# The head norm of a differential attention, its mean squares gathered in eight rows of one bank

## The chip, the cores and the metric

One core of one Trainium2 chip. The metric is device time in microseconds for one execution, the median of several runs. Engines: TensorE (PE, matrix products, results in PSUM banks of 128x512 fp32), VectorE (DVE), ScalarE (ACT), GpSimd (POOL, which doesn't read PSUM), SyncE (SP, which issues the weight transfers).

## The reference

A diffusion block of two parts. The second part has two layers; the change lies in the second of them (the "odd" one), a differential attention over 512 positions and 256 context positions, with 8 heads of 128 columns. Cut to what matters:

```
def rms_norm(x, g):
    xf = x.astype(jnp.float32)
    return (xf * lax.rsqrt(jnp.mean(jnp.square(xf), -1, keepdims=True) + RMS_EPS) * g).astype(x.dtype)

def diff_attend(q, k, v, lam, lambda_init, subln_g):
    s = jnp.einsum('bqhtd,bkhtd->bthqk', q, k) * HEAD_DIM ** -0.5
    p = jax.nn.softmax(s, axis=-1)
    a = p[:, 0] - lam * p[:, 1]
    o = jnp.einsum('bhqk,bkhe->bqhe', a, v)          # 512 positions, 8 heads, 128 columns
    o = rms_norm(o, subln_g) * (1.0 - lambda_init)   # the head norm: mean over a head's 128 columns
    return o.reshape(..., 1024)

o_l = diff_attend(...);  out_l = o_l @ w_out
xl = layer_norm(ALPHA * xl + gt1_l * out_l, ln1_g[i], ln1_b[i])
```

## The kernel before

Activations lie transposed: 128 columns on the partitions, positions along the free dimension. So a head's output is one tile `f.O[:, h, :]` of 128x512 fp32, and the mean over its 128 columns is a sum over partitions, made by TensorE with a constant matrix `m128` (128x128, all 1/128) as stationary operand; the result stands alike in all 128 rows of a bank.

Five programs, one for each engine, are written out by hand (`tensor_odd`, `vector_odd`, `scalar_odd`, `pool_odd`; SP has its own). An instruction counts its engine's semaphore up (`up(name)`), others wait for that count (`at(name)`). `everyone(k, eng, stage)` is a barrier: the engine waits until all four have reached the end of `stage`. PSUM banks are handed out in turn by `k.B.take`; a product that takes a bank waits until its last reader is done.

The stages around the change, in order:

- `tensor_attend`, `vector_attend`, `scalar_attend`: 32 units (8 heads of 4 query tiles), a software pipeline three units deep. VectorE takes the maximum (L2112), ScalarE the exponentials (L2183), VectorE the weighted difference (L2136, L2138), TensorE turns it (L280) and multiplies by the values (L259). After a head's fourth unit ScalarE copies its bank to `f.O` (L2201).
- `odat`, a barrier.
- The head norm, key `odn`. ScalarE squares the eight heads into `f.q1` (L2633). TensorE forms eight means, one bank each (`tensor_norms`, fp32, each product two half-products in the trace). VectorE adds EPS from PSUM into `f.k1` (L797), ScalarE takes the root (L2637), VectorE the reciprocal of 128x512 (L802), scales `f.O` by it and by the gain (L2601). ScalarE casts the result to the high half `f.oh[h]` (L2640), VectorE subtracts to get the low half `f.ol[h]` (L2603). VectorE does these last steps head after head.
- The output projection `dout`, eight projections of eight heads each, three fp32r products a head (high by high L253, low by high L254, high by low L255), 24 in all for each. The first waits for head q's halves before its q-th three. After each projection VectorE adds the result to `k.X` (L1835) and TensorE sums the one before for the layer norm's mean (`X,squares`, L259).
- The layer norm of 128x512: mean, variance, L1761 add, L1776 root, L1765 reciprocal, L1785 and L1788 scaling.

Weights go through a ring of six raw tiles; ScalarE casts the high half of each (L235) and GpSimd subtracts the low half (L243), two projections ahead. During the head norm GpSimd does nothing.

```
def project_in(k, pe, name, x, segs, each=None, among=(0, 1, 2, 3, 4, 5)):
    hi, lo = k.W.pair(name)
    pe.wait_ge(k.W.split(name))
...
        for q in range(8):
            if each is not None:
                pe.wait_ge(each(q))
```

Of the kernel before, what the change touches and what calls it, by code (L numbers as in the profile page):

```python
# [8 lines left out]
F = mybir.dt.float32  # L9
# [15 lines left out]
VECS = [("norm1", 8), ("convw", 80), ("convb", 16), ("ssd_norm", 8), ("hyw", 72), ("hyb", 24), ("hbias", 16),  # L25
        ("hy_norm", 8), ("norm2", 8), ("final_norm", 8), ("bmod", 48), ("dtb", 1), ("hyb1", 1), ("hyb2", 1),
        ("fr0", 1), ("fr1", 1), ("ln1g", 16), ("ln1b", 16), ("ln2g", 16), ("ln2b", 16), ("fcw", 132),
        ("fcb", 44), ("bmod2", 96), ("qn", 2), ("kvn", 1), ("subln", 1), ("c1", 16)]
ROWS = [("alog", 32), ("dskip", 16), ("sink", 8), ("lq1", 64), ("lk1", 64), ("lq2", 64), ("lk2", 64), ("i16", 16)]

SEG2, SEG1 = [(0, 512), (512, 768)], [(0, 512)]
# [226 lines left out]
def mm(e, out, w, x, first=True, last=True):  # L258
    return e.matmul(out, w, x, start=first, stop=last, skip_group_check=True)  # L259
# [23 lines left out]
def everyone(k, eng, stage):  # L283

    eng.wait_ge(k.P.at("end", stage), k.V.at("end", stage), k.A.at("end", stage), k.G.at("end", stage))
# [506 lines left out]
def vector_norms(k, dv, key, groups, out, finish, tiles=None):  # L792
    tiles = tiles or (2 if key == "ssdn" else 1)
    for g in range(groups):
        r = out[:, 512 * g:512 * g + 512]
        dv.wait_ge(k.P.at(key, tiles * g + tiles - 1))
        dv.e.tensor_scalar(r, k.B.of((key, g)), EPS, None, ALU.add).then_inc(*k.V.up(key, "ms", g))  # L797
        k.B.over((key, g), k.V.now())
    for g in range(groups):
        r = out[:, 512 * g:512 * g + 512]  # L800
        dv.wait_ge(k.A.at(key, "sqrt", g))
        dv.e.reciprocal(r, r).then_inc(*k.V.up())  # L802
        dv.wait_ge(k.V.now())
        finish(g, r)

# [1360 lines left out]
            values(i - 3)  # L2168


def scalar_attend(k, ac, at, prepare=None):
    e, P, V, A, B, key = ac.e, k.P, k.V, k.A, k.B, at.key
    N, nP = len(at.units), len(at.P)

# [21 lines left out]
    def values(i):  # L2196
        u = at.units[i]
        if u.last:
            ob = B.of((key, "o", u.key))[u.p0:u.p0 + u.rows, 0:u.width]
            ac.wait_ge(P.at(key, "o", i))  # L2200
            e.copy(u.out[0] if isinstance(u.out, tuple) else u.out, ob).then_inc(*A.up(key, "o", i))  # L2201
            B.over((key, "o", u.key), A.now())

    for i in range(N + 3):
        if prepare and i < N:
# [333 lines left out]
def tensor_odd(k, pe):  # L2539
# [23 lines left out]
    pe.wait_ge([G.at("rot", ("d", j)) for j in range(16)], A.at("Vd", 1, 5))  # L2563
    tensor_attend(k, pe, f.at, lambda i: None)
    P.name("end", "odat")
    everyone(k, pe, "odat")
    tensor_norms(k, pe, "odn", 8, 1, lambda n: f.q1[:, 512 * n:512 * n + 512], k.sq["m128"])
    tensor_residual(k, pe, "res1", "dout", lambda q, s: (f.oh[q], f.ol[q]), SEG1, f.P[1:3], lambda q: V.at("odn", "f", q))
    P.name("end", "res1")


def vector_odd(k, dv):
# [21 lines left out]
    everyone(k, dv, "odin")  # L2594
    vector_attend(k, dv, f.at)
    V.name("end", "odat")
    everyone(k, dv, "odat")

    def finish(h, r):
        o = f.O[:, h, :]  # L2600
        e.scalar_tensor_tensor(out=o, in0=o, scalar=k.sub, in1=r, op0=ALU.mult, op1=ALU.mult).then_inc(*V.up("odn", "o", h))  # L2601
        dv.wait_ge(A.at("odn", "oh", h))
        e.tensor_tensor(f.ol[h], o, f.oh[h].bitcast(F), ALU.subtract).then_inc(*V.up("odn", "f", h))  # L2603

    vector_norms(k, dv, "odn", 8, f.k1, finish)
    vector_residual(k, dv, "res1", "dout", m, 16, SEG1)
    V.name("end", "res1")

# [1 line left out]
def scalar_odd(k, ac):  # L2610
# [15 lines left out]
            B.over(("Vd", hf, c), A.now())  # L2626
    A.name("end", "odin")
    everyone(k, ac, "odin")
    scalar_attend(k, ac, f.at)
    A.name("end", "odat")  # L2630
    everyone(k, ac, "odat")
    for n in range(8):
        e.square(f.q1[:, 512 * n:512 * n + 512], f.O[:, n, :]).then_inc(*A.up("odn", "sq", n))  # L2633
    for g in range(8):
        r = f.k1[:, 512 * g:512 * g + 512]
        ac.wait_ge(V.at("odn", "ms", g))
        e.activation(r, r, AF.Sqrt).then_inc(*A.up("odn", "sqrt", g))  # L2637
    for h in range(8):
        ac.wait_ge(V.at("odn", "o", h))
        e.copy(f.oh[h], f.O[:, h, :]).then_inc(*A.up("odn", "oh", h))  # L2640
# [4 lines left out]
def pool_odd(k, po):  # L2645
    e, W, G, f = po.e, k.W, k.G, k.od
    pool_gain(k, po, "ff0", 768, k.vec["ln2g"][:, 0:8], k.vec["ln2b"][:, 0:8])
    everyone(k, po, "ff0")
    e.dma_start(f.rope, k.d["rope"][:, 1024:2048]).then_inc(*k.rope1l.up())
    W.lo(po, ("dqk", 0))  # L2650
    po.wait_ge(k.rope1l.at())
    for j in range(16):
        if j:
            W.lo(po, ("dqk", j))
        dst = f.q[:, j, :] if j < 8 else f.k[:, j - 8, :]
        pool_rotate(k, po, ("d", j), dst[:, 0:512], f.rope[:, 0:512], f.tmp)
    for j in range(8):
        W.lo(po, ("dv", j))
    G.name("end", "odin")
    everyone(k, po, "odin")  # L2660
    G.name("end", "odat")
    everyone(k, po, "odat")
    for j in range(8):
        W.lo(po, ("dout", j))
    G.name("end", "res1")
# [10 lines left out]
def _cols(v):  # L2676

    return np.ascontiguousarray(np.asarray(v).reshape(-1, 128).T)
# [85 lines left out]
def _arrays(p):  # L2764
# [27 lines left out]
    def taps(w):  # L2792
# [11 lines left out]
         "fcw": np.concatenate([taps(p["ffn_conv_w_2"][i]) for i in range(2)], 1), "fcb": _cols(p["ffn_conv_b_2"]),  # L2804
         "bmod2": _cols(p["b_mod_2"]), "qn": _cols(p["mla_q_norm_2"]), "kvn": _cols(p["mla_kv_norm_2"]),
         "subln": _cols(p["diff_subln_g_2"]), "c1": c2(p["c"], p["c_ctx"])}
    a["vecs"] = np.concatenate([v[n] for n, _ in VECS], 1)
    r = {"alog": p["ssd_a_log"], "dskip": p["ssd_d"], "sink": p["swa_sink_2"], "lq1": p["diff_lam_q1_2"],
         "lk1": p["diff_lam_k1_2"], "lq2": p["diff_lam_q2_2"], "lk2": p["diff_lam_k2_2"],
# [301 lines left out]
```

## Time and profile before

| | us |
|---|---|
| median of 3 runs | 5046.19 (5045.71 to 5047.88) |
| the profiled execution | 5075.65 |
| its span | 5073.8 |
| busy: PE, DVE, ACT, POOL | 4531.9, 2722.1, 1515.6, 1754.2 |
| end of attention's last products to the last three products of projection 0 | 4538.15 to 4590.92 |

The profiled execution takes 0.6% longer than those without a profile. Times in rows are from the start of its span. A TensorE that is called busy isn't one at its peak: the granted clock (1.00 is 2.4 GHz, 0.50 is 1.2 GHz) says how fast its products ran.

### The profile page before, as it was taken

What the parts mean: (1) busy time and instruction counts of PE and PEld (TensorE: products, weight loads), DVE (VectorE), ACT (ScalarE), POOL (GpSimd) and SP (SyncE); (2) the same over time, 40 slices, a digit from 0 to 9 for tenths busy, and PEclk for the clock granted to TensorE, in tenths of its full rate; (3) what the DMA queues carried; (4) which work ended last, traced back from release to release, by engine and by line L of the source; (5) the groups of instructions that cost most, each with busy time, mean ns of one, the idle gap of its engine ahead of it and who ended that gap; (6) DMA issues with size and microseconds to landing.
All of it is one profiled execution on the core that took longest, in us unless ns stands there. A gap on an engine that the chain in (4) does not pass through costs nothing.

```text
span 5073.8 us, 51551 instructions
## 1 busy us (share of the span) xinstructions
PE 4531.9 (89%) x20654; PEld 3503.6 (69%) x20654; DVE 2722.1 (54%) x4692; ACT 1515.6 (30%) x2546; POOL 1754.2 (35%) x933
## 2 busy tenths in 40 slices
PE   7866988787669999999999979997999979986998
PEld 3755845356557888888888856666888857754886
DVE  3875745349887666654443334563443450485334
ACT  3211211034752222222222233443212122343222
POOL 2243432025964444444444421003223225102442
PEclk9987999898789999999999999988999989998999
DMA  5210200121235544444433210001122202101331
GB/s 203 96 67 31 92 29 17 62 72 46 117 155 197 171 161 166 164 155 166 171 136 121 100 37 16 13 1 50 55 63 63 63 29 63 34 1 54 92 96 49
DMA packets 170618, 440.76 MB, mean 87 GB/s; under 512 B 12203, under 2 KB 78955, under 8 KB 167436
## 3 DMA queue, kind: packets, MB, share of 16 engines
q1 hardware_dynamic: 168060, 422.61, 24.5%
q0 software_dynamic: 2320, 14.86, 0.8%
q8 instruction: 164, 2.69, 0.2%
q14 instruction: 74, 0.61, 0.0%
HBM read 401.77 MB, written 35.65 MB: 86 GB/s over the span
## 4 chain that ended last, share of the span: by engine, by line
PE 60%; DVE 7%; ACT 2%; issue 1%; DMA 0%; POOL 0%; DVEq 0%; ACTq 0%; POOLq 0%
PE psum L253 17%; PE psum L255 17%; PE psum L254 17%; PE psum L259 7%; DVE st L2112 2%; PE psum L280 1%; DVE Pd L2138 1%; DVE k L802 1%; DVE X L1785 0%; ACT P L2183 0%; DVE ffl L1725 0%; DVE Pe L2136 0%; DVE rstd L1765 0%; DVE X L1788 0%; DVE st L2119 0%
## 5 line engine op out<-in xcount | busy, mean ns | idle before, releaser
L243 POOL TENSOR_TENSOR pair<-raw_ring,pair 128x1024 fp32r<-128x1024 f32 (+1 forms) x503 | 1243.8, 2488 | 2297.2 <-ACT pair L235 2297.1
L235 ACT CAST pair<-raw_ring 128x1024 fp32r<-128x1024 f32 (+1 forms) x503 | 510.3, 1044 | 370.7 <-PE psum L255 321.7
L253 PE MATMUL psum<-pfh,pair 128*128 128x512 f32 x1152 | 460.0, 399 | 27.4 <-POOL pair L243 25.8
L1578 DVE SCALAR_TENSOR_TENSOR h<-psum,mods,h 128x512 f32<-128x512 f32 x512 | 373.0, 748 | 184.4 <-PE psum L255 182.9
L255 PE MATMUL psum<-pfh,pair 128*128 128x512 f32 x1152 | 458.8, 398 | 0.0
L254 PE MATMUL psum<-pfl,pair 128*128 128x512 f32 x1152 | 458.4, 398 | 0.0
L253 PE MATMUL psum<-ffh,pair 128*128 128x512 f32 (+1 forms) x1056 | 382.3, 362 | 45.3 <-DVE ffl L1725 45.3
L253 PE MATMUL psum<-Ah,pair 128*128 128x512 f32 x1024 | 408.6, 399 | 9.8 <-DVE h L1578 4.8
L255 PE MATMUL psum<-Ah,pair 128*128 128x512 f32 x1024 | 407.9, 398 | 0.0
L254 PE MATMUL psum<-Al,pair 128*128 128x512 f32 x1024 | 407.8, 398 | 0.0
L254 PE MATMUL psum<-ffl,pair 128*128 128x512 f32 (+1 forms) x1056 | 380.3, 360 | 0.0
L255 PE MATMUL psum<-ffh,pair 128*128 128x512 f32 (+1 forms) x1056 | 379.8, 360 | 0.0
L1636 ACT ACTIVATE gl<-psum 128x512 f32<-128x512 f32 x122 | 73.1, 599 | 832.6 <-PE psum L255 832.6
L1571 DVE TENSOR_TENSOR pr<-gl,Gb 128x512 f32<-128x512 f32 x128 | 91.4, 714 | 342.2 <-ACT gl L1636 324.3
L253 PEld LDWEIGHTS psum<-pfh,pair 128*128 128x128 f32 x1152 | 218.7, 190 | 79.3 <-issue 23.1
L259 PE MATMUL psum<-o,o 128*128 128x128 f32 x1024 | 177.1, 339 | 101.6 <-POOL o L1503 77.2
L253 PEld LDWEIGHTS psum<-ffh,pair 128*128 128x128 f32 x1056 | 200.6, 190 | 84.1 <-issue 39.1
L254 PEld LDWEIGHTS psum<-pfl,pair 128*128 128x128 f32 x1152 | 218.8, 190 | 50.5
L255 PEld LDWEIGHTS psum<-pfh,pair 128*128 128x128 f32 x1152 | 218.6, 190 | 50.5
L259 PEld LDWEIGHTS psum<-o,o 128*128 128x128 f32 x1024 | 161.4, 243 | 117.6 <-POOL o L1503 78.5
L1948 DVE SCALAR_TENSOR_TENSOR X<-psum,mods,X 128x512 f32<-128x512 f32 (+1 forms) x264 | 170.8, 661 | 121.0 <-PE psum L255 121.0
L253 PEld LDWEIGHTS psum<-Ah,pair 128*128 128x128 f32 x1024 | 194.4, 190 | 56.3 <-issue 9.6
(517 smaller groups left out, 9305.0 us busy)
## 6 DMA issues: line engine op xcount, KB each, us to landing
raw_ring<-wmod SPq DMA_DIRECT2D x144, 512.0 KB, 5.2
raw_ring<-peeru SPq DMA_DIRECT2D x128, 512.0 KB, 4.2
raw_ring<-peerv SPq DMA_DIRECT2D x128, 512.0 KB, 4.8
gates<-stage SPq DMA_DIRECT2D x16, 2048.0 KB, 6.4
Gb<-gates SPq DMA_DIRECT2D x32, 1024.0 KB, 9.2
raw_ring<-win SPq DMA_DIRECT2D x48, 512.0 KB, 4.4
raw_ring<-wgate SPq DMA_DIRECT2D x44, 512.0 KB, 3.5
raw_ring<-wup SPq DMA_DIRECT2D x44, 512.0 KB, 3.6
```

Of the source, the lines that this page charges most:

```text
L235: ac.e.copy(self.pair(t)[0], k.R.of(t)).then_inc(*k.A.up("hi", t))
L243: po.e.tensor_tensor(lo, k.R.of(t), hi.bitcast(F), ALU.subtract).then_inc(*k.G.up("lo", t))
L253: e.matmul(out, w[0], x[0], start=first, stop=False, skip_group_check=True)
L254: e.matmul(out, w[0], x[1], start=False, stop=False, skip_group_check=True)
L255: return e.matmul(out, w[1], x[0], start=False, stop=last, skip_group_check=True)
L259: return e.matmul(out, w, x, start=first, stop=last, skip_group_check=True)
L280: return e.transpose(out, src, k.sq["ident"][0:n, 0:n])
L1571: e.tensor_tensor(v3(y, 32), v3(x, 32), G4[:, :, n % 4, :], ALU.mult).then_inc(*V.up("act", n))
L1578: e.scalar_tensor_tensor(out=h[:, j, :], in0=B.of(("down", gi, j)), scalar=m[:, 40 + j, 0:1], in1=h[:, j, :], op0=ALU.mult, op1=ALU.add).t ...
L1636: e.activation(gelus(k, n), B.of((("U", n), 0)), AF.Gelu).then_inc(*A.up("gelu", n))
L1948: e.scalar_tensor_tensor(out=x, in0=B.of((key, "down", gi, q, s))[:, 0:b - a], scalar=m[:, 40 + q, s:s + 1], in1=x, op0=ALU.mult, op1=ALU. ...
L2112: e.tensor_reduce(s[:, 0:1], bank[:, 0:u.n], AX, ALU.max).then_inc(*V.up())
```

## The change

The mean squares of the eight heads are gathered in one bank. The stationary operand for head h is a window of 8 columns out of a table `z128` (128x15, 1/128 in column 7, else 0), so that the sum lands in row h and adds nothing to the other rows; eight products accumulate into 8x512. Then one add, one root and one reciprocal of 8x512 instead of eight each of 128x512. A second product for each head brings row h back to all 128 rows: its stationary operand is column h of the first eight rows of the unit matrix, broadcast to 128 columns (8x128). VectorE scales `f.O` straight from that bank. The low half of odd heads goes to GpSimd. The squares of a head are issued in the attention's loop, behind the head's copy. The barrier `odat` falls. The means and the products with ones take banks 0 to 5. The constants `z64`, `z256`, `z128` add 52 columns to the transfer of `vecs`; only `z128` is read.

```diff
+def tensor_means(k, pe, key, n, sq, place, rows, among=(0, 1, 2, 3, 4, 5, 6, 7)):
+    bank = k.B.take((key, "ms"), 1, among)
+    pe.wait_ge(k.B.free((key, "ms")))
+    for i in range(n):
+        pe.wait_ge(k.A.at(key, "sq", i))
+        mm(pe.e, bank[0:rows, :], place(i), sq(i), i == 0, i == n - 1).then_inc(*k.P.up(key, "sq", i))
+
+def vector_means(k, dv, key, n, rows, out):
+    dv.wait_ge(k.P.at(key, "sq", n - 1))
+    dv.e.tensor_scalar(out[0:rows, :], k.B.of((key, "ms"))[0:rows, :], EPS, None, ALU.add).then_inc(*k.V.up(key, "ms"))
+    k.B.over((key, "ms"), k.V.now())
+
+def scalar_means(k, ac, key, rows, out):
+    ac.wait_ge(k.V.at(key, "ms"))
+    ac.e.activation(out[0:rows, :], out[0:rows, :], AF.Sqrt).then_inc(*k.A.up(key, "sqrt"))
+
+def vector_inverse(k, dv, key, rows, out):
+    dv.wait_ge(k.A.at(key, "sqrt"))
+    dv.e.reciprocal(out[0:rows, :], out[0:rows, :]).then_inc(*k.V.up(key, "inverse"))
+
+def tensor_back(k, pe, key, g, w, out, among=(0, 1, 2, 3, 4, 5, 6, 7)):
+    bank = k.B.take((key, "back", g), 1, among)
+    pe.wait_ge(k.V.at(key, "inverse"), k.B.free((key, "back", g)))
+    mm(pe.e, bank, w, out).then_inc(*k.P.up(key, "back", g))

@@ scalar_attend, in values(i), at a head's last unit
             B.over((key, "o", u.key), A.now())
+            if square:
+                square(u.key)

@@ tensor_odd
-    everyone(k, pe, "odat")
-    tensor_norms(k, pe, "odn", 8, 1, lambda n: f.q1[:, 512 * n:512 * n + 512], k.sq["m128"])
-    tensor_residual(k, pe, "res1", "dout", lambda q, s: (f.oh[q], f.ol[q]), SEG1, f.P[1:3], lambda q: V.at("odn", "f", q))
+    tensor_means(k, pe, "odn", 8, lambda h: f.q1[:, 512 * h:512 * h + 512], lambda h: k.vec["z128"][:, 7 - h:15 - h], 8, SIX)
+    for h in range(8):
+        tensor_back(k, pe, "odn", h, k.sq["ident"][0:8, h:h + 1].to_broadcast([8, 128]), f.k1[0:8, 0:512], SIX)
+    tensor_residual(k, pe, "res1", "dout", lambda q, s: (f.oh[q], f.ol[q]), SEG1, f.P[1:3], lambda q: (G if q % 2 else V).at("odn", "f", q))

@@ vector_odd
-    everyone(k, dv, "odat")
-
-    def finish(h, r):
+    vector_means(k, dv, "odn", 8, 8, f.k1[:, 0:512])
+    vector_inverse(k, dv, "odn", 8, f.k1[:, 0:512])
+
+    def second(h):
+        dv.wait_ge(A.at("odn", "oh", h))
+        e.tensor_tensor(f.ol[h], f.O[:, h, :], f.oh[h].bitcast(F), ALU.subtract).then_inc(*V.up("odn", "f", h))
+
+    for h in range(8):
         o = f.O[:, h, :]
-        e.scalar_tensor_tensor(out=o, in0=o, scalar=k.sub, in1=r, op0=ALU.mult, op1=ALU.mult).then_inc(*V.up("odn", "o", h))
-        dv.wait_ge(A.at("odn", "oh", h))
-        e.tensor_tensor(f.ol[h], o, f.oh[h].bitcast(F), ALU.subtract).then_inc(*V.up("odn", "f", h))
-
-    vector_norms(k, dv, "odn", 8, f.k1, finish)
+        dv.wait_ge(P.at("odn", "back", h))
+        e.scalar_tensor_tensor(out=o, in0=o, scalar=k.sub, in1=B.of(("odn", "back", h)), op0=ALU.mult, op1=ALU.mult).then_inc(*V.up("odn", "o", h))
+        B.over(("odn", "back", h), V.now())
+        if h % 2:
+            second(h - 1)

@@ scalar_odd
-    scalar_attend(k, ac, f.at)
+
+    def square(h):
+        ac.wait_ge(A.now())
+        e.square(f.q1[:, 512 * h:512 * h + 512], f.O[:, h, :]).then_inc(*A.up("odn", "sq", h))
+
+    scalar_attend(k, ac, f.at, square=square)
     A.name("end", "odat")
-    everyone(k, ac, "odat")
-    for n in range(8):
-        e.square(f.q1[:, 512 * n:512 * n + 512], f.O[:, n, :]).then_inc(*A.up("odn", "sq", n))
-    for g in range(8):
-        r = f.k1[:, 512 * g:512 * g + 512]
-        ac.wait_ge(V.at("odn", "ms", g))
-        e.activation(r, r, AF.Sqrt).then_inc(*A.up("odn", "sqrt", g))
+    scalar_means(k, ac, "odn", 8, f.k1[:, 0:512])

@@ pool_odd
-    everyone(k, po, "odat")
+    for h in range(1, 8, 2):
+        po.wait_ge(k.A.at("odn", "oh", h))
+        e.tensor_tensor(f.ol[h], f.O[:, h, :], f.oh[h].bitcast(F), ALU.subtract).then_inc(*G.up("odn", "f", h))
     for j in range(8):
         W.lo(po, ("dout", j))

@@ constants
+        ("z64", 30), ("z256", 7), ("z128", 15)]
+    v["z128"] = np.tile(np.arange(15) == 7, (128, 1)) / 128.0
```

## Rows read from the trace of the kernel before

**Rows 1.** The page: shares of the chain that ended last, by engine.
```profile
PE 60%; DVE 7%; ACT 2%; issue 1%; DMA 0%; POOL 0%; DVEq 0%; ACTq 0%; POOLq 0%
```

**Rows 2.** Chain of waits, 4500 to 4660 us: start, length, engine, tile, line.
```profile
4535.46 2.69 PE psum L259 x24
4538.18 0.59 ACT O L2201
4538.86 0.64 ACT q L2633
4539.63 7.12 PE psum L259 x16
...
4547.47 3.27 DVE k L802
4550.76 0.76 DVE O L2601
4551.55 0.63 ACT oh__32736_512_387 L2640
4552.19 0.69 DVE ol L2603
...
4590.92 0.79 PE psum L253
...
4592.56 0.43 PE psum L253
...
4599.86 0.86 PE psum L259 x2
...
4606.30 0.86 PE psum L259 x2
...
4649.72 0.70 DVE rstd L1761
...
4651.11 3.35 DVE rstd L1765
```

**Rows 3.** Windows: length, then busy PE, PEld, DVE, ACT, POOL; PEclk; DMA.
```profile
4551.00:4553.00 2.00, 0.00 (x0) 0.00 (x0) 1.32 (x3) 0.62 (x1) 0.00 (x0) 0.71 0.00 0
4596.00:4597.00 1.00, 1.00 (x5) 0.78 (x5) 0.00 (x0) 0.00 (x0) 0.49 (x1) 0.89 0.73 287
4653.00:4660.00 7.00, 0.00 (x0) 0.00 (x0) 6.92 (x10) 5.40 (x7) 2.75 (x3) 0.59 0.00 0
40.30:45.50 5.20, 5.20 (x7) 0.85 (x8) 2.98 (x9) 0.90 (x1) 0.00 (x0) 0.50 0.08 31
4663.00:4672.00 9.00, 3.85 (x7) 2.16 (x8) 8.96 (x5) 3.41 (x5) 9.00 (x5) 0.50 0.43 123
```

**Rows 4.** Timeline of ScalarE, in the attention and at the kernel's end.
```profile
4526.66 0.60 ACT L2201 COPY O<-psum 128x512 f32<-128x512 f32 x1
4528.92 0.90 ACT L2183 ACTIVATE Pd<-psum,st 128x768 f32<-128x768 f32 x1 [1.66 <-DVE st L2119]
...
5056.40 1.28 ACT L1776 ACT_TABLE_LOAD   x1
5058.32 0.63 ACT L1776 ACTIVATE rstd<-rstd 128x512 f32<-128x512 f32 x1 [0.64 <-DVE rstd L1761]
```

**Rows 5.** Timeline of TensorE, 0 to 45 us; "128*2" is the stationary operand.
```profile
40.30 5.28 PE L259 MATMUL psum<-raw_ring,vecs 128*2 128x512 f32 x6 [5.59 <-ACT vecs L495]
```

**Rows 6.** Groups of instructions, DVE and POOL: count, busy us, mean ns.
```profile
L2155 DVE TENSOR_TENSOR efl<-psum,efh 64x512 fp32r<-64x512 f32 x16 | 11.0, 689 | 20.8 <-ACT efh L2201 20.8
...
L2232 POOL TENSOR_TENSOR k<-k,rope 128x512 f32<-128x512 f32 x8 | 10.3, 1293 | 34.2 <-PE psum L259 34.2
...
L243 POOL TENSOR_TENSOR pair<-raw_ring,pair 128x1024 fp32r<-128x1024 f32 (+1 forms) x503 | 1243.8, 2488 | 2297.2 <-ACT pair L235 2297.1
```

**Rows 7.** Transfers by issuing queue: KB each, us to landing.
```profile
vecs<-vecs POOLq DMA_DIRECT2D x1, 328.5 KB, 8.8
```

**Rows 8.** Timeline of VectorE, 4660 to 4680 us.
```profile
4662.98 8.97 DVE L1725 TENSOR_TENSOR ffl<-hid,ffh 128x512 fp32r<-128x512 f32 x4
```

More of the change, by code:

```diff
@@ L27 @@
         ("fr0", 1), ("fr1", 1), ("ln1g", 16), ("ln1b", 16), ("ln2g", 16), ("ln2b", 16), ("fcw", 132),
-        ("fcb", 44), ("bmod2", 96), ("qn", 2), ("kvn", 1), ("subln", 1), ("c1", 16)]
+        ("fcb", 44), ("bmod2", 96), ("qn", 2), ("kvn", 1), ("subln", 1), ("c1", 16),
+        ("z64", 30), ("z256", 7), ("z128", 15)]
 ROWS = [("alog", 32), ("dskip", 16), ("sink", 8), ("lq1", 64), ("lk1", 64), ("lq2", 64), ("lk2", 64), ("i16", 16)]
@@ L2168, in vector_attend, with scalar_attend @@
             values(i - 3)
-def scalar_attend(k, ac, at, prepare=None):
+def scalar_attend(k, ac, at, prepare=None, square=None):
     e, P, V, A, B, key = ac.e, k.P, k.V, k.A, k.B, at.key
@@ L2806, in _arrays @@
          "subln": _cols(p["diff_subln_g_2"]), "c1": c2(p["c"], p["c_ctx"])}
+    p2 = np.arange(128)[:, None] // 64
+    v["z64"] = (np.arange(30)[None] == 14 + p2) / 64.0
+    v["z256"] = np.tile(np.arange(7) == 3, (128, 1)) / 256.0
+    v["z128"] = np.tile(np.arange(15) == 7, (128, 1)) / 128.0
     a["vecs"] = np.concatenate([v[n] for n, _ in VECS], 1)
```

## The prediction

> **What bounds the kernel now.** I read the page first: TensorE carries 60% of the chain over the whole span [rows 1], so a change to one norm matters most where TensorE stands still. The chain of waits from 4535 to 4660 us shows such a place [rows 2]. The last products of attention end at 4538.15 (4535.46 + 2.69). Then come the copy of O, the squares, sixteen half-products of means (7.12), and eight rounds, one a head, of reciprocal 3.27, scaling 0.76, cast 0.63 and subtraction 0.69 on the chain; they begin at 4547.47, and at 4590.92, 5.43 us a round later, the last three products of projection 0 begin (they need head 7). From the end of attention's products to 4590.92 are 52.8 us, 1% of the span, and VectorE's reciprocals hold more than half of them. The windows then show what TensorE's clock did [rows 3]: full (2.4 GHz) through the means, granted half (1.2 GHz) from about 4551.8 (0.71 mean in 4551 to 4553), and full again at about 4596.2 (0.89 in 4596 to 4597), 5.3 us after gapless work began.
>
> **The change part by part.** Each sum is measured from the end of attention's products.
>
> *Squares in attention.* Seven of eight move into the loop. After the copy of O at the end of a head (0.60) ScalarE stands 1.66 us before the next exponential [rows 4]. The wait for its own copy (0.09 between 4538.77 and 4538.86 [rows 2]) and the square (0.64) take 0.73 of it, 0.93 are left: nothing on the path. If that cover were gone, seven times 0.73 would cost 5 us. The eighth square ends at 4539.5.
>
> *Means.* TensorE need not stand for the first square: the eight products follow attention's at once, and the eighth square is there long before the eighth product is. That is 7.12 instead of 8.59 (4546.74 − 4538.15). The stationary matrix has 8 columns instead of 128, but the products stream 512 columns; the nearest row, stationary matrices of 2 columns, took 0.88 us a half-product at half clock [rows 3, 5], twice the 0.445 of the means at full clock [rows 2]. So a narrow matrix saves nothing.
>
> *One add, one root, one reciprocal.* From the add to the start of the reciprocal the layer norm took 1.39 us, and the reciprocal 3.35 (4649.72 to 4654.46 [rows 2]). With 0.03 to start: 4.77. Are eight rows cheaper than 128? A subtraction over 64 partitions took 689 ns [rows 6], as long as the 0.69 over 128 [rows 2]: time goes by columns. I take 3.35; the other end, 3.1 us less, stays for the range. The load of the Sqrt table, 1.28 us, is issued ahead of the wait: at the kernel's end it ran at 5056.40, before the root was released at 5058.32 [rows 4]. Here it lies beside the means. Its cost if it came behind the wait: 1.28.
>
> *Products with ones.* Eight more fp32 products of 512 columns. TensorE starts 0.06 after the reciprocal; the first takes about 1.0 at full clock, hand-over 0.1: 1.2 us. At 0.89 each the rest stay ahead of VectorE, which needs 0.76 for a scaling and, for each pair, 0.69 for one subtraction. The six banks suffice: the seventh product waits for the first scaling only.
>
> *Scalings and subtractions.* On VectorE 8 × 0.76 + 3 × 0.69 = 8.2 until head 7 is scaled. Its cast: 0.67. Then GpSimd's subtraction: 0.1 to start (hand-overs in rows 2 take 0.03 to 0.09), 1.29 by the nearest row [rows 6], 0.05 to TensorE: 1.4.
>
> Sum: 7.12 + 4.77 + 1.2 + 8.2 + 0.67 + 1.4 = 23.4 against 52.8: **29.4 us less**.
>
> *Clock in the first two projections.* Before, 27 products took 8.94 us (4590.92 to 4599.86); at full clock 24 take 6.44 − 0.86 = 5.58, and 27 take 6.3 [rows 2]. After the change TensorE has worked almost without gap for 11 us by then, so it should be at full clock: 2.6 less, of which I keep 0.2 for a product's start: 2.4.
>
> *Where work is moved past.* GpSimd now has four subtractions ahead of the low halves of `dout`. That for projection 2 (2.49 [rows 6]) begins at about 23.6 and ends at 26; TensorE needs it at 23.4 + 6.3 + 0.9 = 30.6. Nothing. ScalarE's casts keep their place behind `oh`. Behind the new wait of the root stand the casts `oh`, which need its result anyway; behind the seventh product with ones stands projection 0, which needs all eight; the barrier `odat` that falls held nobody but TensorE and the squares. SP's queue is not touched; no transfer ran in the norm. The vectors grow by 52 columns, 26 KB, at the start: 328.5 KB landed in 8.8 us [rows 7], so at most 0.7 later for what is behind them; I take 0.1, since the larger x lies between them and the first product.
>
> *DVE and GpSimd at once.* While GpSimd worked (9 of 9 us [rows 3]), four subtractions of two SBUF tiles took 8.97 us, 2.24 each instead of 0.69 [rows 8]. Here VectorE's subtraction starts right behind the odd scaling and ends 0.69 later; GpSimd's begins 0.8 after the scaling and ends at 2.1; the next subtraction on VectorE is due at 0.69 + 1.52 = 2.2. They miss each other narrowly. I take 0; three full collisions would cost 3.9.
> The Trainium skill, SBUF — State Buffer, "SBUF: two separate sides", calls this an exclusive lock that a VectorE instruction with two SBUF inputs and a GpSimd one hold for their whole length, the other being blocked. The trace agrees (2.24 against 0.69); scaling from PSUM has one SBUF input and would be free of it. The rule speaks against this edit, and by it the sum would be the same as long as the two alternate as above.
>
> Total: 29.4 + 2.4 − 0.1 for the start of the kernel = 31.7; the narrow miss on the shared port may cost 0.1 a pair, so I take **31.4 us**. The profiled execution took 5075.65 us (span 5073.8, 1.85 around it), 0.6% over the 5046.19 median; scaled, 31.4 is 31.2. Forecast: 5015.0 us.
>
> **Rivals.**
> 1. *The clock is half when the products with ones begin.* TensorE stands 4.8 us ahead of them (7.12 to 11.95). The clock fell 5.1 us after the means ended, and 4.6 us after the layer norm's last product (0.59 over 4653 to 4660 [rows 3]), on both sides of 4.8. At half clock a product takes 1.7 [rows 5], three fit into the 5.3 us [rows 3], and the third scaling is 1.9 us late. Gain 29.3: 5017.
> 2. *The clock stays half through all eight*: 13.7 us of products, the last scaling 5.2 later, and the 2.2 of the projections gone. Gain 24: 5022. Against it: 4596.2 came 5.3 us after gapless work began. For it: no product with 8 rows is in the trace.
> 3. *VectorE and GpSimd collide*: three times 1.29. Gain 27.5: 5018.7.
> 4. *Reciprocal, root and add are cheaper on eight rows*: gain 34.5: 5011.8.
> 5. *Squares force a change of tables in the loop.* Two loads of 1.28 and 0.73 against 1.66 of idle time: 1.63 a head, 11.4 over seven. Gain 20: 5026. Against it: squares ran 0.09 us after the copy, behind exponentials, and a load came only before Sqrt [rows 2, 4].
> The Trainium skill, ScalarE: Activation LUTs, "What ACT_TABLE_LOAD costs", puts a switch at 1283 ns plus a drain of about 1380. The load agrees (1.28); with the drain this rival would take some 30 us and cancel the gain. No drain is seen here.
> 6. *Slower: half clock through the whole output projection.* A product with 8 of 128 rows may not bring the clock back, and nothing after it would. Half clock costs 0.43 against 0.2325 a product [rows 2]: 15 more in projection 1 (+3.0), six projections (+28.4), eight means and eight variances at +0.86 each (+13.8), rival 2's 5.2: +50 against 29.3, 5067 us. It decides if the clock is still half in about the fifth projection, after some 60 us of such work; the trace had 5.3.
> 7. *The gain is given back later* (weights late, another stage's clock): within 0.2%. The slack of 4.6 us above speaks against it.
>
> **How the numbers follow.** Chances: forecast 0.44, rival 1 0.28, rival 2 0.06, rival 3 0.08, rival 4 0.05, rival 5 0.03, rival 6 0.02, rival 7 0.04. About 0.2% (10 us) is what a measurement of this kernel tells from no change. Faster by more: forecast and rivals 1 to 5, 0.94; within: 0.04; slower: 0.02. The range 5011 to 5020 takes in the forecast and rivals 1, 3 and 4, 0.85 in all, with the runs' scatter of about 1 us at each end; rival 2 lies outside.
>
> **What would show it.** In the profile after: eight squares among the exponentials, the next exponential still released by VectorE; eight mean products right behind attention's; one reciprocal of 8x512, 3.35 us; the windows' clock over the eight products with ones, and their spacing (0.86 or 1.7); VectorE's four subtractions 0.69 each; GpSimd's four near 1.3; `dout`'s last three products some 23 us behind attention's end; projection 1 at 0.23 a product. The prediction is wrong if attention's loop is longer, if products with ones set the pace of the scalings, or if GpSimd's last subtraction is late.

## The result, and the profile after

| us | before | after |
|---|---|---|
| median, range (4 runs each) | 5047.03 (5045.71 to 5048.19) | 4990.72 (4984.73 to 4993.35) |
| ratio, 95% interval | | 0.9883 (0.9870 to 0.9896) |
| the profiled execution, its span | 5075.65, 5073.8 | 4993.35, 4991.5 |

The medians lie 56.3 us apart, 1.12%; by the ratio, which isn't formed from these two medians alone, the gain is 1.17%, 59 us. Gains in us below are differences of medians. The forecast was 5015.0, a gain of 31.2; 4990.72 lies outside its range of 5011 to 5020. The direction was right, the size was not. What follows shows that the 56.3 are two things: some 23 us from the head norm, less than forecast, and over 30 us from a move of most tiles by 192 bytes, which the prediction did not see.

In the kernel after, lines stand 1 to 43 further down than before: the products are L254 to L256 and L260, the reciprocal is L832, the scaling L2644. The chain of waits of the kernel after, around the norm (start, length, engine, tile, line), answers to [rows 2]:

```profile
4480.95 9.90 PE psum L260 x40
4490.87 0.69 DVE k L821
4491.58 0.64 ACT k L827
4492.24 3.35 DVE k L832
4495.63 14.02 PE psum L260 x16
4509.65 0.72 PE psum L254
4510.37 0.43 PE psum L255
...
4515.07 0.43 PE psum L254
4515.49 0.27 PE psum L255
4516.68 0.23 PE psum L254
```

Attention's last product ends at 4483.86, and its end is the zero of all stage times below. The eight means follow it at once inside the piece of 9.90 us. Then come add, root and one reciprocal, 4.76 us together. Instead of eight rounds with a reciprocal each there is one block of 14.02 us: the eight products with ones, at 1.75 us each. They, not VectorE's scalings, set the pace, and the products of projection 0 behind them still take 0.43 us each until about 4515.3, then 0.23.

Windows of the kernel after (columns as in [rows 3]; the column behind POOL's is the granted clock):

```profile
4485.00:4491.00 6.00, 5.83 (x14) 1.08 (x12) 0.13 (x1) 1.43 (x2) 0.00 (x0) 1.00 0.00 0
4491.00:4495.60 4.60, 0.00 (x0) 0.00 (x0) 3.88 (x2) 0.63 (x1) 0.00 (x0) 0.93 0.00 0
4495.60:4509.60 14.00, 13.97 (x17) 5.17 (x17) 7.04 (x10) 4.32 (x7) 3.80 (x3) 0.50 0.00 1
4509.60:4515.30 5.70, 5.70 (x15) 4.44 (x15) 1.35 (x2) 2.62 (x4) 3.66 (x2) 0.50 0.00 0
4515.50:4518.00 2.50, 2.50 (x12) 2.05 (x12) 0.00 (x0) 0.00 (x0) 0.00 (x0) 1.00 0.69 205
```

The clock is full through the means, whose stationary operand has 8 columns and all 128 rows. It falls late in TensorE's pause, about 4 us after the means (0.93 is the mean over 4.6 us of which the last part is at half). It is then half for 14.0 us although TensorE is busy for 13.97 of them, and comes back only after 5.7 us of the projection.

Timelines of ScalarE, VectorE and GpSimd of the kernel after (start, length, line, operation, out and in, in brackets the idle time before and who ended it). ScalarE:

```profile
4471.11 0.60 ACT L2235 COPY O<-psum 128x512 f32<-128x512 f32 x1
4471.74 0.63 ACT L2674 ACTIVATE q<-O 128x512 f32<-128x512 f32 x1
4473.37 0.90 ACT L2217 ACTIVATE Pd<-psum,st 128x768 f32<-128x768 f32 x1 [1.00 <-DVE st L2153]
...
4485.16 1.28 ACT L827 ACT_TABLE_LOAD   x1
4491.58 0.63 ACT L827 ACTIVATE k<-k 8x512 f32<-8x512 f32 x1 [5.13 <-DVE k L821]
```

VectorE:

```profile
4490.87 0.68 DVE L821 TENSOR_SCALAR k<-psum 8x512 f32<-8x512 f32 x1 [9.46 <-PE psum L260]
4492.24 3.34 DVE L832 RECIPROCAL k<-k 8x512 f32<-8x512 f32 x1 [0.69 <-ACT k L827]
...
4499.45 0.75 DVE L2644 SCALAR_TENSOR_TENSOR O<-O,sub,psum 128x512 f32<-128x512 f32 x1 [0.96 <-PE psum L260]
4500.11 0.68 DVE L2639 TENSOR_TENSOR ol<-O,oh__32784_512_387 128x512 fp32r<-128x512 f32 x1
```

GpSimd:

```profile
4504.34 1.27 POOL L2705 TENSOR_TENSOR ol<-O,oh__34320_512_390 128x512 fp32r<-128x512 f32 x1 [2.06 <-ACT oh__34320_512_390 L2681]
```

The square in attention's loop is hidden: the next exponential is still released by VectorE, with 1.00 us left of 1.66 [rows 4]. The load of the Sqrt table lies beside the means and nobody waits for it. The reciprocal on 8 rows costs what it costs on 128, 3.35 [rows 2]. Each scaling waits for a product with ones. VectorE's subtraction takes 0.68 and GpSimd's 1.27: they do not meet.

The norm and its wait are over by 4516. The other part of the gain is not in this stage at all. In windows of 500 us in the middle of the first part, where nothing of the change runs, TensorE is busy all the time at full clock in both kernels. Before:

```profile
2000.00:2500.00 500.00, 500.00 (x2145) 405.00 (x2144) 284.07 (x397) 139.56 (x179) 225.01 (x88) 1.00 0.48 162
```

After:

```profile
2000.00:2500.00 500.00, 500.00 (x2208) 414.01 (x2207) 287.86 (x404) 143.57 (x184) 235.53 (x93) 1.00 0.50 169
```

The same products come 63 more often in the same time: 233.1 ns from one to the next before, 226.4 after. Part of that distance is the execution that was profiled before: at 5075.65 it is 29 us longer than that kernel's median. The first experiment's control separates this.

### The profile page after: what moved, and what is told of

Same layout as the page of the kernel before. It is cut to its first block, busy times and chain, and to the rows that moved or that the text cites. A ratio compares the mean times of both kernels' runs of the same rounds, so it can differ in the third digit from the quotient of the medians.

```text
span 4991.5 us, 51556 instructions
## 1 busy us (share of the span) xinstructions
PE 4475.2 (90%) x20670; PEld 3489.7 (70%) x20670; DVE 2688.9 (54%) x4674; ACT 1512.0 (30%) x2539; POOL 1759.2 (35%) x937
## 4 chain that ended last, share of the span: by engine, by line
PE 60%; DVE 7%; ACT 2%; issue 1%; DMA 0%; POOL 0%; DVEq 0%; ACTq 0%; POOLq 0%
PE psum L254 17%; PE psum L255 17%; PE psum L256 17%; PE psum L260 7%; DVE st L2146 2%; PE psum L281 1%; DVE Pd L2172 1%; DVE X L1819 0%; ACT P L2217 0%; DVE ffl L1759 0%; DVE Pe L2170 0%; DVE rstd L1799 0%; DVE X L1822 0%; DVE st L2153 0%; DVE efl L2189 0%
## 5 line engine op out<-in xcount | busy, mean ns | idle before, releaser
L254 PE MATMUL psum<-pfh,pair 128*128 128x512 f32 x1152 | 451.7, 392 | 27.1 <-POOL pair L244 26.1
L256 PE MATMUL psum<-pfh,pair 128*128 128x512 f32 x1152 | 449.5, 390 | 0.0
L254 PE MATMUL psum<-ffh,pair 128*128 128x512 f32 (+1 forms) x1056 | 377.3, 357 | 45.7 <-DVE ffl L1759 45.7
L254 PE MATMUL psum<-Ah,pair 128*128 128x512 f32 x1024 | 400.8, 391 | 10.2 <-DVE h L1612 4.9
L256 PE MATMUL psum<-Ah,pair 128*128 128x512 f32 x1024 | 400.0, 391 | 0.0
L256 PE MATMUL psum<-ffh,pair 128*128 128x512 f32 (+1 forms) x1056 | 376.3, 356 | 0.0
L254 PEld LDWEIGHTS psum<-pfh,pair 128*128 128x128 f32 x1152 | 217.2, 189 | 73.6 <-issue 22.5
L260 PE MATMUL psum<-o,o 128*128 128x128 f32 x1024 | 173.8, 335 | 104.7 <-POOL o L1537 75.5
L254 PEld LDWEIGHTS psum<-ffh,pair 128*128 128x128 f32 x1056 | 200.6, 190 | 82.9 <-issue 39.1
L256 PEld LDWEIGHTS psum<-pfh,pair 128*128 128x128 f32 x1152 | 217.1, 188 | 45.4
L260 PEld LDWEIGHTS psum<-o,o 128*128 128x128 f32 x1024 | 158.7, 239 | 120.2 <-POOL o L1537 78.2
L254 PEld LDWEIGHTS psum<-Ah,pair 128*128 128x128 f32 x1024 | 193.4, 189 | 51.6 <-issue 10.6
```

The source lines that it names most:

```text
L254: e.matmul(out, w[0], x[0], start=first, stop=False, skip_group_check=True)
L256: return e.matmul(out, w[1], x[0], start=False, stop=last, skip_group_check=True)
```

## The experiments

Two questions: where do the 33 us come from that the norm can't give, and what does the norm give by itself? Beside each of them the kernel before ran on the same chip, with medians of 5046.61 to 5047.95 us over 11 to 21 executions. Not all experiments had the same chip, so each ratio is to the kernel before beside it.

### The control, and the 52 columns alone

*Control: the kernel before, unchanged.*

> The kernel before, unchanged, for a profile on the same chip as the runs beside it. Ratio 1.000. The first profile of it took 5075.65 us, 29 over the median of the runs without one. If that excess belonged to that one execution, this profile takes 5045 to 5050, and products of 512 columns in the experts' stage are spaced less than the 0.2333 us of the first profile, nearer to the 0.2267 of the changed kernel. If it belongs to the profile, it takes 5070 to 5080 again.

Measured: 5053.31 us (8 runs), ratio 1.0009 (0.9986 to 1.0033). Its own profiled execution took 5047.48 us and has this window:

```profile
2000.00:2500.00 500.00, 500.00 (x2186) 410.29 (x2185) 287.45 (x402) 141.42 (x181) 234.03 (x92) 1.00 0.50 170
```

That is 228.7 ns a product. So two profiled executions of the kernel before have two product spacings, 229 ns (5047 us) and 233 ns (5075 us), and the one profiled for the prediction was the slower. The spacing of the kernel after, 226.4, is below both.

This execution, whose span is 5045.6 us, can be laid beside that of the kernel after (4991.5). Timelines of the control: TensorE's last products of attention, and VectorE's add behind the variance of the layer norm.

```profile
4507.15 2.84 PE L259 MATMUL psum<-PTd,Vd 128*128 128x128 f32 x24
...
4621.55 0.69 DVE L1761 TENSOR_SCALAR rstd<-psum 128x512 f32<-128x512 f32 x1 [4.27 <-PE psum L259]
```

The same add in the kernel after:

```profile
4572.90 0.69 DVE L1795 TENSOR_SCALAR rstd<-psum 128x512 f32<-128x512 f32 x1 [4.26 <-PE psum L260]
```

Attention's products end at 4509.99 in the control and at 4483.86 in the kernel after: 26.1 us are gained before the new norm has begun. From there to the add it is 111.56 against 89.04, 22.5 us less, and behind it 5.5 us less. That is the whole difference of 54.1 us, split without any further kernel.

*The 52 columns without the norm.* The new norm is left out; only the constants are added, which nobody reads.

```diff
-        ("fcb", 44), ("bmod2", 96), ("qn", 2), ("kvn", 1), ("subln", 1), ("c1", 16)]
+        ("fcb", 44), ("bmod2", 96), ("qn", 2), ("kvn", 1), ("subln", 1), ("c1", 16),
+        ("z64", 30), ("z256", 7), ("z128", 15)]
```

> The kernel before with nothing of the change but the 52 more columns of constants, which move every tile behind them by 48 columns (192 bytes a partition). Theory A (the head norm gained only about 22 us, the rest of the 56 comes from the new places of the tiles): 5047 - 34 = 5013, ratio 0.993, and the experts' products are closer together than in the control. Theory B (all of the gain comes from the head norm and from what follows it): 5047, ratio 1.000.

Measured: 5005.56 us (5 runs, 5003.17 to 5022.0), ratio 0.9914 (0.9885 to 0.9942): 42.4 us less, from columns that are transferred and not read. Its window:

```profile
2000.00:2500.00 500.00, 500.00 (x2208) 414.01 (x2206) 287.51 (x404) 143.60 (x184) 235.57 (x93) 1.00 0.50 169
```

The products are as dense as in the kernel after. The constants lie first in SBUF, and the base of the tiles behind them is rounded up, so these move up by 48 columns (192 bytes a partition). The raw tiles and the weight pairs hang from the other end and stay.

*The move without the columns.*

```diff
+    m.at += 48          # ahead of k.base = m.at
```

> The kernel before with its tiles moved by the same 48 columns, but with the constants' transfer as it was (no more bytes, no other places in HBM). Theory A with SBUF addresses as its cause: as the kernel with 52 more columns, ratio 0.993. Theory A with the placement in HBM as its cause: ratio 1.000, and only the kernel with more constants gains. Theory B: ratio 1.000.

Measured: 5016.09 us (5 runs), ratio 0.9924 (0.9899 to 0.9949); 2207 products in the same window. Nothing but addresses in SBUF differs from the kernel before, so the place is the cause of this gain, and neither the transfer nor its contents. Whether the columns add anything to it isn't told: the intervals of the two kernels overlap.

*The norm without the move.* The kernel after, with `z128` taken at the end of the odd layer's tiles and written by GpSimd, and no columns added to `vecs`.

```diff
-        ("z64", 30), ("z256", 7), ("z128", 15)]
+    f.z128 = m.take("z128", 15)
...
+    e.memset(f.z128, 0.0).then_inc(*G.up())
+    po.wait_ge(G.now())
+    e.memset(f.z128[:, 7:8], 1.0 / 128).then_inc(*G.up("z128"))
```

> The changed kernel with every tile at its old place: the table of the windows is filled by two memsets of GpSimd at the start of the odd layer, in free columns behind its tiles, and the three new constants are not transferred. Theory A: the head norm's own gain alone, 5047 - 22 = 5025, ratio 0.9956. Theory B: as the changed kernel, 4991, ratio 0.988.

Measured: 5025.13 us (9 runs), ratio 0.9950 (0.9934 to 0.9965). The norm alone gains 22.8 us (25 by the ratio), with an interval of 18 to 33 us (0.35% to 0.66% of 5048). The execution that was profiled, 5060.44 us, is its slowest, and has the long spacing, as the one before:

```profile
2000.00:2500.00 500.00, 500.00 (x2144) 405.02 (x2143) 283.77 (x396) 139.62 (x179) 226.25 (x89) 1.00 0.48 161
```

Its stage is that of the kernel after: products with ones from 11.77 to 25.78 us behind attention, half clock from 10.7 to 31.2. Move alone and norm alone sum to 31.9 + 22.8 = 54.7 or, with the other kernel that has only the move, 42.4 + 22.8 = 65.2. The 56.3 measured for both lies between. With nothing left over beyond the scatter, move and norm together account for the gain.

### Which distance, and between what?

The move shifts most tiles, but not the ring of weight pairs `pair`, which hangs from the other end of SBUF. So the distance between a product's stationary operand (`pair`) and its moving operand (`Ah`, `Al`, `pfh`, `pfl`) changes, as it does to every other tile that moved. That can be reached from the other side: leave all tiles and move only the pairs down by 48 columns.

```diff
-        m.at = 53184 - 6 * 1024 - 2048 * (s + 1)
+        m.at = 53184 - 6 * 1024 - 2048 * (s + 1) - 48
```

> The kernel before with only the weight tiles (the eight pairs of high and low halves) moved, 48 columns down, so that weights and moving operands stand as far apart as in the kernel moved by 48 columns, but every moving operand in its old place. Theory F (the moving operand's own address): spacing stays 0.2292 in the experts' stage, ratio 1.000. Theory H (the distance between the two operands of a product): spacing 0.2267, ratio 0.993.

Measured: 5010.89 us (2 runs), ratio 0.9919 (0.9888 to 0.9950). The window:

```profile
2000.00:2500.00 500.00, 500.00 (x2207) 414.17 (x2206) 287.33 (x405) 143.39 (x184) 235.59 (x93) 1.00 0.51 169
```

The gain is there with no activation moved. So what counts is how far the pairs lie from the tiles behind the constants. The groups by shape in this window show which instructions the gain is in. The control, whose spacing is the usual one of the kernel before:

```profile
L254 PE MATMUL psum<-pfl,pair 128*128 128x512 f32 x360 | 141.8, 394 | 0.0
L253 PE MATMUL psum<-pfh,pair 128*128 128x512 f32 x361 | 141.5, 392 | 0.0
L255 PE MATMUL psum<-pfh,pair 128*128 128x512 f32 x361 | 140.1, 388 | 0.0
```

The kernel with the pairs moved (its other groups read 389 too):

```profile
L253 PE MATMUL psum<-pfh,pair 128*128 128x512 f32 x368 | 143.2, 389 | 0.0
```

The same products, fp32r of 512 columns, have means of 394, 392 and 388 ns, 391 together, against 389 (their length in the pipeline, which is more than the distance to the next). There is no idle time in either; the products themselves are 2 ns shorter on average.

*Only the activations of the first part moved*: `Ah`, `Al` and their neighbours, by 48 columns; `pfh` and `pfl` stay.

```diff
-    m.at = low
+    m.at = low + 48
```

> The kernel before, with only the second set of tiles of the experts' stage moved by 48 columns (Ah, Al, gl, pr, Gb, crow, junk), every other tile in its old place. Theory F (the spacing of products goes by the address of the moving operand): products of Ah and Al are spaced 0.2267 us, those of pfh and pfl stay at 0.229 to 0.233; 3072 products by 2.6 to 6.7 ns, 8 to 20 us won, ratio 0.996 to 0.998. Theory G (something common to the whole kernel shifted with the base): ratio 1.000 and no spacing changes.

Measured: 5049.87 us (8 runs), ratio 1.0004 (0.9994 to 1.0015), 2191 products in the window against the control's 2186. By the starts in the timelines of that window, products that read `Ah` and `Al` came every 227.7 ns on average instead of 228.9, and those that read `pfh` and `pfl` every 229.2 instead of 228.9. That is half of the way to 226.6, and no gain shows in the whole. If only the distance between a product's own two operands counted, those of `Ah` and `Al` should have come at 226.6. So that the moving operand is the tile that matters is supported in part and not shown.

### The period

Every kernel below is the kernel before with the tiles behind the constants moved by so many columns of 4 bytes; constants, raw tiles and pairs stay. The expectations were written in three groups, each when the results of the group before were known.

> The kernel before with all tiles behind the constants moved by 16 columns (64 bytes a partition), so that they begin on a multiple of 128 bytes, as with 48 columns. Theory F1 (what counts is the place modulo 128 bytes): as with 48 columns, spacing 0.2267, ratio 0.993. Theory F2 (it goes by a larger distance): another spacing.

> The kernel before with all tiles behind the constants moved by 32 columns (128 bytes a partition). 16 columns made it slower (1.0037) and 48 faster (0.992). If the spacing goes down steadily with the shift, 32 is in between, near 1.000; if it goes by a residue modulo 128 bytes it is as without a shift, 1.000 with 0.2292; anything else says that a larger distance counts.

> The kernel before with all tiles behind the constants moved by 80 columns, so that they begin on a multiple of 1024 bytes a partition. If good places are those on large powers of two: spacing 0.2267 or less and ratio 0.992 or less. If 80 is a place like any other: between 0.992 and 1.004, and the gain at 48 was luck.

> The kernel before with all tiles behind the constants moved by 40 columns (160 bytes a partition). So far 0 columns gave 2186 products in the window 2000 to 2500 us, 16 and 32 gave 2153 and 2145, 48 gave 2207, 80 gave 2153. If 48 is the middle of a broad good range: 2190 or more and a ratio under 0.997. If it is a narrow one (48 alone): about 2150, ratio 1.001 to 1.004.

> The same with 56 columns (224 bytes). Broad good range: 2190 products or more, ratio under 0.997. Narrow: about 2150, ratio above 1.

> The same with 64 columns (256 bytes). If the spacing repeats every 256 bytes: as without a shift, 2186 (or 2145 in the slower of its two kinds of execution), ratio 1.000. If it doesn't, anything else; below 0.992 it would be a better place than the change's.

> The same with 112 columns, 48 + 64. If the spacing repeats every 256 bytes: as with 48, 2207 products, ratio 0.992. If not, the good distance is one place in a longer pattern; between 0.992 and 1.004.

| moved by | median, us (runs) | ratio (95%) | products in 2000 to 2500 us |
|---|---|---|---|
| 0 (control) | 5053.31 (8) | 1.0009 (0.9986 to 1.0033) | 2186 |
| 16 | 5065.55 (8) | 1.0037 (1.0027 to 1.0048) | 2153 |
| 32 | 5058.33 (8) | 1.0014 (1.0002 to 1.0027) | 2145 |
| 40 | 5076.79 (3) | 1.0057 (1.0035 to 1.0080) | 2145 |
| 48 | 5016.09 (5) | 0.9924 (0.9899 to 0.9949) | 2207 |
| 56 | 5088.09 (2) | 1.0084 (1.0054 to 1.0113) | 2145 |
| 64 | 5048.15 (8) | 1.0004 (0.9993 to 1.0015) | 2186 |
| 80 | 5065.43 (8) | 1.0028 (1.0015 to 1.0040) | 2153 |
| 112 | 5013.43 (3) | 0.9914 (0.9862 to 0.9966) | 2207 |

The pairs (0, 64), (16, 80) and (48, 112) agree, in products and nearly in time: over the distances run, what counts repeats with 64 columns, 256 bytes. A period of 128 bytes would have made 16 like 48, and it costs 0.4% where 48 gains 0.8%. Inside the period 48 is narrow: 40 and 56, 32 bytes to each side, are the slowest, 0.6% and 0.8% over the kernel before. The window of the slowest, moved by 56:

```profile
2000.00:2500.00 500.00, 500.00 (x2145) 401.65 (x2144) 284.39 (x396) 137.90 (x177) 225.56 (x89) 1.00 0.48 163
```

and of that moved by 112:

```profile
2000.00:2500.00 500.00, 500.00 (x2207) 414.15 (x2207) 287.70 (x404) 143.64 (x184) 235.51 (x93) 1.00 0.51 169
```

As means over the window, 500 us by the count, three ranges of spacing appear: 226.6 ns (48, 112, the pairs moved), 228.7 (0, 64) and 232.2 to 233.1 (16, 32, 40, 56, 80). The count of this one window doesn't order the slow kernels: 32, 40 and 56 have 2145 each and lie 30 us apart, so something outside this window adds to it.

### The clock in the norm

Two edits to the kernel after, alone and together. *Filler*: five products of squares by `m128` into a bank that nobody reads, between the means and the products with ones, so that TensorE's pause is filled.

```diff
+def warm(k, pe, key, x, n):
+    bank = k.B.take((key, "warm"), 1, SIX)
+    pe.wait_ge(k.B.free((key, "warm")))
+    for i in range(n):
+        mm(pe.e, bank, k.sq["m128"], x)
+    k.B.over((key, "warm"))
...
+    warm(k, pe, "odn", f.q1[:, 0:512], 5)
```

> The changed kernel with five more products of 512 columns (m128 by the squares, into a bank that nobody reads) between the means and the wait for the reciprocal; 4.3 us of work in a gap of 4.8. Theory C (the clock fell in the gap and the eight-row products were slow for that alone): the products with ones are spaced 0.89 us instead of 1.75, projection 0 ends about 9 us sooner, ratio to before 0.9883 - 0.0018 = 0.9865. Theory D (eight-row products don't hold the clock, whatever stood before them): full at first, half again within 8 us, and at most 4 us are won. Theory E (they are slow by themselves): nothing is won, or the 0.3 us by which the filler is late is lost.

Measured: 4989.45 us (4 runs), ratio 0.9890 (0.9874 to 0.9907). TensorE's timeline in that kernel ("8*128" is the stationary operand, rows by columns):

```profile
4475.89 7.03 PE L260 MATMUL psum<-q,vecs 128*8 128x512 f32 x16
4482.85 4.56 PE L260 MATMUL psum<-q,squares 128*128 128x512 f32 x10
4487.73 11.26 PE L260 MATMUL psum<-k,squares 8*128 8x512 f32 x16 [0.32 <-DVE k L832]
```

and its windows:

```profile
4487.00:4490.00 3.00, 2.68 (x7) 1.05 (x7) 1.68 (x3) 0.33 (x1) 0.00 (x0) 1.00 0.00 0
4491.00:4499.00 8.00, 8.00 (x11) 2.71 (x9) 4.95 (x8) 3.24 (x6) 3.80 (x3) 0.50 0.01 2
```

The pause is down to 0.32 us and the products with ones begin at full clock. The clock still falls 2.8 us later, with TensorE busy without a gap. So the pause is not what keeps the clock down: these products of 8 rows don't hold it.

*All 128 rows*: the same result (the unit matrix's column is 0 outside row h) from a stationary operand of 128 rows.

```diff
-        tensor_back(k, pe, "odn", h, k.sq["ident"][0:8, h:h + 1].to_broadcast([8, 128]), f.k1[0:8, 0:512], SIX)
+        tensor_back(k, pe, "odn", h, k.sq["ident"][:, h:h + 1].to_broadcast([128, 128]), f.k1[:, 0:512], SIX)
```

> The changed kernel with the products with ones made over 128 rows instead of 8: the stationary operand is the same column of the whole unit matrix (row h ones, the others zero), the moving one has 128 rows, of which the lower 120 are old finite values that meet zeros; the output is the same. Nothing fills the gap. Theory D: 128 rows bring the clock back about 5 us after they begin, as fp32r products of 128 rows did before (5.3) and after the change (5.8); the eight take some 10 us instead of 14.0, 3 to 4 us won, ratio 0.9876. Theory C and E: the eight take 14.0 us and the clock rises behind them as before.

Measured: 4989.32 us (4 runs), ratio 0.9882 (0.9865 to 0.9898). TensorE's timeline:

```profile
4500.75 8.53 PE L260 MATMUL psum<-k,squares 128*128 128x512 f32 x16 [4.81 <-DVE k L832]
```

and windows:

```profile
4500.00:4503.00 3.00, 2.25 (x3) 1.17 (x4) 0.83 (x2) 0.00 (x0) 0.00 (x0) 0.53 0.00 0
4503.50:4520.00 16.50, 16.50 (x62) 11.45 (x61) 8.23 (x13) 8.53 (x13) 9.95 (x6) 1.00 0.16 38
```

The pause is as long as in the kernel after, the clock is half when the products begin, and it is full again within 3 us of their start. Same pause, same columns, same number of products; only the rows differ, of the stationary and of the moving operand at once. Which of the two matters isn't told apart.

*Both.*

> The changed kernel with both edits: five filler products in the gap and the products with ones over 128 rows. In their own runs the first kept the clock full for 3 us more and the second brought it back 3.4 us after it fell. Theory D (only products of many rows hold the clock): the clock never falls, the eight products with ones take 7 to 8 us (now paced by VectorE), and projection 0 and 1 end some 10 us sooner than in the changed kernel (39.5 us after attention's end), at about 29.5; ratio to before 0.9883 - 0.0020 = 0.9863. If the filler alone had done what could be done: 36.5. The time of a whole run may hide it, since its scatter is 5 us; the stage's own times decide.

Measured: 4987.22 us (5 runs, 4977.83 to 4990.8), ratio 0.9868 (0.9846 to 0.9890). TensorE's timeline and the window:

```profile
4499.27 7.13 PE L260 MATMUL psum<-k,squares 128*128 128x512 f32 x16 [0.32 <-DVE k L832]
```

```profile
4487.50:4520.00 32.50, 32.18 (x101) 17.22 (x102) 13.65 (x16) 13.25 (x19) 11.36 (x7) 1.00 0.11 33
```

The clock is full throughout. Stage times in us behind attention's last product, from the timelines:

| kernel | products with ones | projection 0 begins | projection 1 is through | clock half |
|---|---|---|---|---|
| before | none | 14.9 (its first three) | 61.6 | about 13.7 to 58.1 |
| after | 11.8 to 25.8 | 25.7 | 39.5 | 11.1 to 31.6 |
| norm without the move | 11.8 to 25.8 | 25.7 | 39.5 | 10.7 to 31.2 |
| filler | 11.8 to 23.0 | 23.0 | 36.5 | 14.6 to 28.3 |
| 128 rows | 11.8 to 20.3 | 19.7 | 31.1 | 11.2 to 14.6 |
| both | 11.8 to 18.9 | 18.3 | 29.7 | never |

The stage is 9.8 us shorter with both than in the kernel after. In the whole time the difference to it, 3.5 us, is not told apart from none, since the times of kernels with this placement scatter over some 10 us. It is the shortest median of all kernels run.

## Why the prediction was wrong in size

**The step that failed first.** "The vectors grow by 52 columns, 26 KB, at the start ... I take 0.1" priced the transfer and nothing else. The transfer did cost about this little: the first square came 0.27 us later, at 18.44 and not 18.17. But the columns also move the tiles behind them by 192 bytes, and that gave 31.9 us (tiles moved), 36.6 (pairs moved, 2 runs) and 42.4 (columns alone), each with an interval clear of zero. The sum had no term for it and no rival was about it. Nothing in one trace of before could have given the amount. What could have been seen is that the move reaches every product that reads a weight pair; they are 14,784 of 20,654 in the trace of before, 12,144 of them with 512 columns. An estimate: 2.1 ns on each (228.7 to 226.6) are 26 us for those of 512 columns and 31 for all. That the profile's own execution was 0.6% over the median was noticed and scaled away; it was the other product spacing of the same placement (2145 products in the window against 2186), a first sign that this spacing isn't fixed.

**The second step: the clock over the products with ones.** The forecast had them at full clock, 0.44 to rival 1's 0.28 and rival 2's 0.06. Rival 2 is what happened: half clock through all eight, 14.0 us where it said 13.7, so that the products with ones set the pace of the scalings, which the prediction had named as a sign of being wrong. Its gain of 24 agrees with the norm's own 22.8, whose interval is 18 to 33; the stage of the kernel with the norm alone is 61.6 − 39.5 = 22.1 shorter. What half clock costs can be read from the kernel with both edits, which has none: from the first product with ones to the first of projection 0 it is 13.95 us against 6.57, and from there through projection 1 13.8 against 11.4; 7.4 + 2.4 = 9.8, which is 39.5 − 29.7. "4596.2 came 5.3 us after gapless work began" was used against rival 2, but those 5.3 us were products with 128 rows. The argument for rival 2, "no product with 8 rows is in the trace", was the better one and got too little weight. Even without the move the forecast would have missed: the norm alone ran at 5025.13, above 5020. The two errors have opposite signs, so that the forecast's gain of 31.2 lies between the 22.8 of the norm and the 56.3 of the whole.

**What held.**
- *Squares in attention*: nothing on the path, 1.00 us of idle time left (predicted 0.93).
- *Means*: 7.03 for 7.12, at full clock with 8 columns.
- *Add, root, reciprocal*: 4.76 for 4.77, and 8 rows cost as much as 128. Rival 4 is out.
- *Table*: one load, 1.28 us, beside the means. Rival 5 is out, and the drain of about 1380 ns that the Trainium skill, ScalarE: Activation LUTs, "What ACT_TABLE_LOAD costs", adds to a load can't be seen here, since the load ends 5 us before the root starts.
- *VectorE and GpSimd at once*: 0.68 and 1.26 to 1.29, no collision. But in the kernel after the products with ones held the two apart. The kernel with both edits is the proper test: there VectorE works without a gap (two scalings and a subtraction in 2.05 us) and GpSimd's four still take 1.27 to 1.30, the first three in the main beside VectorE's two scalings, the last behind all of VectorE's work. The first runs 0.15 us into a subtraction of VectorE's, which took 0.70 even so. So rival 3 is out at the predicted pace as well. The lock that the Trainium skill, SBUF — State Buffer, "SBUF: two separate sides", describes was avoided and not disproved.
- *Rival 6*: the clock came back after 5.7 us of the projection, not after 60, so it is out.
- *Rival 7*: the add behind the variance comes 22.5 us earlier against attention's end (111.57 and 89.04), so nothing was given back by then.

**The sum at full clock.** 23.4 to the last three products of projection 0 and 6.3 more to the end of projection 1 give 29.7; the kernel with both edits measures 29.73. One reason differs from the text: there TensorE itself is the bound (GpSimd's last subtraction ends 22.6 us behind attention, the product that needs it begins at 23.6). VectorE's chain, which the text summed, is 1 us shorter than what holds.

**What stays open.** Why the distance between the pairs and the other tiles counts, beyond the facts of the table: it repeats with 256 bytes, 192 is good, 160 and 224 are bad. Residues that weren't run, 8 and 24 among them, may be good too. Why the old placement has executions of two kinds, 229 and 233 ns, with the same addresses. Why moving only `Ah` and `Al` brought their products half of the way to the short spacing, and no more. And the norm's 22.8 us rest on a kernel whose nine runs scatter more (5022.76 to 5060.44) than the stage in the trace does, so the trace's 22 is the surer number.

## What to carry to other kernels

When a change adds or resizes a tile ahead of others, it moves them all. Before a gain or loss is put down to the change, run the kernel before with only the move, and the change with the old addresses; here the move alone gave 31.9 to 42.4 us, where move and norm together gave 56.3. Where a product needs only a few rows, give it all 128 with zeros in the stationary operand if the work around it lives by TensorE's full clock: it costs nothing in columns and here shortened the stage by 8.4 us in one trace of each, though the times of the whole kernel, 4989.32 and 4990.72, don't tell it.

## What the runs showed of the hardware

- *The spacing of full-clock products depended on where tiles lie.* fp32r products of 128x128 by 128x512 came every 226.6, 228.7 or 232 to 233 ns on average, by the distance in a partition between the weight pairs and the tiles behind the constants; moves that differ by 256 bytes gave the same. The Trainium skill, TensorE: Matmul & The Clock Gate, "Back-to-back issue gap", gives N / 2.4 + 2.5 ns at full clock for an isolated product, 215.8 for 512 columns, and about 131 ns as sustained, and says nothing of addresses. The measurement decides: no mean here was below 226.
- *TensorE busy for 13.97 of 14.00 us with 8-row products stayed at a granted clock of 0.50.* With 128 rows in the same place it was at 1.00 within 3 us. Products with 8 columns and 128 rows kept 1.00 for 7 us. A full row of "busy" in the profile doesn't tell the clock.
- *A VectorE reciprocal of 512 fp32 columns takes 3.35 us on 8 rows as on 128.*
